# The last expert's down matrix in four loads, its token products moved, and four unread products ahead of the first wait

## What is computed

```python
def expert_choice_ffn(h, router_w, wg, wu, wd):
    ...
    a = jnp.einsum('becd,edf->becf', xs, wg)
    u = jnp.einsum('becd,edf->becf', xs, wu)
    o = jnp.einsum('becf,efd->becd', jax.nn.silu(a) * u, wd) * gate[..., None].astype(h.dtype)
    ...
for l in range(DEPTH):
    ...
    x = x + merged @ w_out[l]
    x = x + expert_choice_ffn(rms_norm(x, norm2_w[l]), router_w[l], ...)
```

## Time and profile before

| | |
|---|---|
| median of 3 runs | 2001.66 us (2000.48 to 2001.76) |
| profiled execution, its own time | 2003.29 us |
| its span, first to last instruction | 2001.5 us |
| mean granted TensorE clock | 0.891 of full |
| PE busy | 1563.8 us, 78% of the span |
| moved by DMA | 644.57 MB, 322 GB/s over the span |

### The profile page before, as it was taken

The page is one execution under the profiler, slowest core; times in us unless marked ns, Lnnn a source line. Parts: engine busy times, 40 slices in busy tenths (PEclk is TensorE's granted clock), DMA queues, the critical chain, the costliest instruction groups (busy, mean ns, idle before and its releaser), DMA issues.

```text
span 2001.5 us, 22268 instructions
## 1 busy us (share of the span) xinstructions
PE 1563.8 (78%) x9588; PEld 879.5 (44%) x9588; DVE 560.0 (28%) x1073; ACT 286.2 (14%) x600; POOL 45.7 (2%) x24
## 2 busy tenths in 40 slices
PE   8999999876576665676799999998765765666767
PEld 5687688432232232222256877884222221322322
DVE  3654771211111111111136547712111111111211
ACT  3233210110000000000132332101100100000010
POOL 0300000000000000000002000000000000000000
PEclk9999999898788887888899999998886878877888
DMA  7522055699999999999966221545999999999998
GB/s 294 227 89 84 1 230 206 250 393 425 432 428 433 435 427 434 434 430 411 423 218 231 85 84 40 237 181 244 437 431 426 432 436 428 430 434 430 431 419 341
DMA packets 26135, 644.57 MB, mean 322 GB/s; under 512 B 2864, under 2 KB 3888, under 8 KB 6320
## 3 DMA queue, kind: packets, MB, share of 16 engines
q1 hardware_dynamic: 24976, 638.47, 75.7%
q10 hardware_dynamic: 1056, 4.53, 0.8%
HBM read 641.94 MB, written 1.05 MB: 321 GB/s over the span
## 4 chain that ended last, share of the span: by engine, by line
PE 51%; DMA 45%; issue 1%; DVE 1%; ACT 1%; DVEq 0%; SPq 0%; ACTq 0%
DMA region<-w_down_dram 41%; PE ps L872 10%; PE ps L487 7%; PE ps L554 6%; PE ps L694 6%; DMA region<-w_down_last_dram 3%; PE ps L767 3%; PE ps L824 2%; PE ps L515 2%; PE ps L677 1%; PE ps L630 1%; PE ps L577 1%; PE ps L532 1%; PE ps L666 1%; PE ps L814 1%
## 5 line engine op out<-in xcount | busy, mean ns | idle before, releaser
L824 PE MATMUL ps<-ring,region 128*32 128x384 f32 (+1 forms) x2944 | 292.1, 531 | 184.9 <-DMA ring<-w_gbu_dram 184.9
L872 PE MATMUL ps<-region,late 128*32 128x512 f32 x1320 | 205.2, 742 | 124.1 <-DMA region<-w_down_dram 121.3
L824 PEld LDWEIGHTS ps<-ring,region 128*32 128x32 f32 x2944 | 120.1, 123 | 351.7 <-DMA ring<-w_gbu_dram 202.3
L487 PE MATMUL ps<-xnT,ring 128*128 128x256 f32 x768 | 178.3, 380 | 4.3 <-DVE region L1148 2.6
L1486 DVE TENSOR_TENSOR region<-region,ps 128x256 f32<-128x256 f32 x32 | 13.5, 421 | 549.7 <-PE ps L824 549.7
L872 PEld LDWEIGHTS ps<-region,late 128*32 128x32 f32 x1320 | 50.9, 133 | 257.5 <-issue 156.5
L487 PEld LDWEIGHTS ps<-xnT,ring 128*128 128x128 f32 x768 | 140.7, 190 | 23.8 <-DVE region L1148 4.4
L890 PE MATMUL ps<-region 128*128 128x512 f32 x256 | 124.3, 617 | 27.7 <-ACT region L1128 21.6
L554 PE MATMUL ps<-xnT,ring 128*128 128x256 f32 x512 | 115.8, 381 | 0.0
L1500 DVE TENSOR_TENSOR x<-x,ps 128x512 f32<-128x512 f32 x128 | 88.0, 688 | 83.0 <-PE ps L890 83.0
L1497 DVE COPY region<-ps 128x512 f32<-128x512 f32 x32 | 22.1, 692 | 314.8 <-PE ps L872 314.2
(11 more groups left out here) (204 smaller groups left out, 1482.1 us busy)
## 6 DMA issues: line engine op xcount, KB each, us to landing
region<-w_down_dram SPq DMA_DIRECT2D x28, 5632.0 KB, 32.9
ring<-w_gbu_dram SPq DMA_DIRECT2D x30, 4928.0 KB, 32.7
region<-w_ga_dram SPq DMA_DIRECT2D x14, 6336.0 KB, 36.8
ring<-w_ga_dram SPq DMA_DIRECT2D x12, 6336.0 KB, 34.8
ring<-units_dram SPq DMA_DIRECT2D x28, 2048.0 KB, 8.4
region<-units_dram SPq DMA_DIRECT2D x6, 2048.0 KB, 12.1
ring<-w_ga_dram SPq DMA_DIRECT2D x2, 4288.0 KB, 13.6
region<-w_down_dram SPq DMA_DIRECT2D x4, 2048.0 KB, 10.7
```

The costliest lines, as they stand in the source:

```text
L487: m = mm(bank(b % 2, S), unit8(n)[:, i, j * P:(j + 1) * P], xnT[:, i], start=i == 0, stop=i == DB - 1)
L824: m = mm(bank(b, QW[j], rows=CAP, row0=CAP * j), xs[:, i, q * CAP:(q + 1) * CAP], w[i][:, j * FT:j * FT + QW[j]], start=i == 0, stop=i == ...
L872: m = mm(bank(c, rows=CAP, row0=CAP * j), hT[:, b * P + CAP * j:b * P + CAP * (j + 1)], wd[:, CT * b + j, c * 512:(c + 1) * 512], start=b ...
```

## The change

The 11 tiles of half 0 arrive in two loads, of 6 and 5 tiles, and PE waits for the second one between its sixth and seventh tile. The 8 and 3 tiles of half 1 arrive as before, under other semaphores (`wd_in[2]`, `wd_end_in`). The token products of half 0 stand after tile 4 of half 1 and no longer after tile 7. Four products of a constant by the identity, 128x256 each, into a PSUM bank that nobody reads again for this expert, stand ahead of the waits for `hT_dve` and for the first load.

```diff
-                        for b, (c0, c1) in enumerate(((0, NF_TILES), (NF_TILES, 2 * NF_TILES - 3), (2 * NF_TILES - 3, 2 * NF_TILES))):
+                        for c0, c1, arrived in ((0, 6, wd_in[0]), (6, NF_TILES, wd_in[1]),
+                                                (NF_TILES, 2 * NF_TILES - 3, wd_in[2]),
+                                                (2 * NF_TILES - 3, 2 * NF_TILES, s["wd_end_in"])):
                             cols = slice(c0 * HW, c1 * HW)
-                            sp.dma_start(R[:, cols], w_down_last[L, :, cols]).then_inc(wd_in[b], 16)
+                            sp.dma_start(R[:, cols], w_down_last[L, :, cols]).then_inc(arrived, 16)
...
                         m.then_inc(s["hT_psum"], 1)
+                        if last and q == GROUP - 1:
+                            for _ in range(4):
+                                mm(bank(3, S), ident, cst[:, 0:S], start=True, stop=True)
 
                         pe.wait_ge(s["hT_dve"], n + 1)
...
-                    tiles(0, 0, NF_TILES).then_inc(s["o_half_psum"], 1)
+                    tiles(0, 0, 6)
                     pe.wait_ge(wd_in[1], 16 * (L + 1))
-                    tiles(1, 0, NF_TILES - 3)
+                    tiles(0, 6, NF_TILES).then_inc(s["o_half_psum"], 1)
+                    pe.wait_ge(wd_in[2], 16 * (L + 1))
+                    tiles(1, 0, 5)
                     pe.wait_ge(s["gselT_act"], n + 1)
                     pe.wait_ge(s["o_act"], n + 1 + FREE)
                     for t in range(SB):
                         to_tokens(n, t, t, 0)
-                    pe.wait_ge(wd_in[2], 16 * (L + 1))
+                    tiles(1, 5, NF_TILES - 3)
+                    pe.wait_ge(s["wd_end_in"], 16 * (L + 1))
                     tiles(1, NF_TILES - 3, NF_TILES).then_inc(s["o_psum"], 1)
```

More of the change, by code:

```diff
@@ L232, in build @@
         wd_last = R[:, 0:NF_TILES * D].rearrange("p (c r d) -> p c r d", c=2, r=NF_TILES)
-        names = """one_dve consts_in dft_in vec_in fvec_in qkw_in filt_in decay_in wqb_in wgbu_in wga_third_in wu_tail_in out_done
+        names = """one_dve consts_in dft_in vec_in fvec_in qkw_in filt_in decay_in wqb_in wgbu_in wga_third_in wu_tail_in wd_end_in out_done
         norm1_rms r_dve r2_dve xT_psum xw_dve xw_act r_psum xnT_dve lat_psum lat_rms lat_ready latT_psum latT_dve latT_act
```

## The result

The changed kernel took 2005.14 us (median of 20 runs, 2000.40 to 2010.47), the kernel before 2001.30 us (median of 20, 1996.29 to 2003.50): ratio 1.002, 95% interval 1.0013 to 1.0027. 3.84 us slower was measured, 3.35 forecast. The runs of the changed kernel spread over 10 us, those of before over 7.

A forecast was written before the change was run, and what follows sets the result against it. The experts are paced by the weights' DMA; each layer's end is set by half 1's arrival and PE's work behind it. 0.85 + 0.1 + 1.6 + 0.8 = 3.35 us on the median 2001.66 gave 2005.0 us, range 2001.6 to 2007.4.

The forecast's parts named there:

- The four loads cost nothing in the stream: Last expert's down loads: first six tiles land 3.1 us earlier, half 1 lands as before; cost 0.
- Rival 3: Load stream, last expert: the cut load brings half 1 1.4 us later per layer, 2007.8 us in all; chance 0.03.
- The unread products: Ahead of half 0: four products take 1.73 us at full clock, hold the tiles back 1.2 us, cost nothing at the end.
- The extra round: Behind half 1's arrival: four rounds of tiles for three, + 0.855 us, 5.70 in all; + 0.85 us in layer 0.
- Rival 4: Behind half 1's arrival: the two rounds of tiles 5 to 10 overlap, layer 1 gains 0.7 us, 2000.9; chance 0.03.
- Layer 1's + 0.1: Behind half 1's arrival in layer 1: 5.58 us before, 5.70 after at full clock, so + 0.1 us.
- Where the stall goes: PE's stall moves between half 0 and half 1, 2.7 to 3.1 us; lost clock then costs 1.6 (layer 1), 0.8 (layer 0).
- the clock is full throughout in both layers: Sign that the forecast is wrong; it expected half clock between half 1's arrival and DVE's copy in at least one layer.
- rival 1: The clock survives both stalls between the halves; only the round is left, 2001.66 + 0.95 = 2002.6 us; chance 0.22.
- 1.6 and 0.8: Us of clock loss behind half 1's arrival: 1.6 in layer 1, 0.8 in layer 0, where the stall is shorter.
- The sum: Both layers' ends: 0.85 + 0.1 + 1.6 + 0.8 = 3.35 us, added to the median 2001.66.

The follow-up runs named there:

- the second profile: Profile from an unedited repeat: of the kernel before (2001.09 us) under Layer 1's + 0.1, of the changed kernel (2005.01 us) under Where the stall goes.
- filler: Six more unread 128x256 products put into the changed kernel between half 0's last tile and the wait for half 1; 1998.65 us with them in both layers.

## Why the prediction was right, step by step

- **The four loads cost nothing in the stream.** Right. The gap from the first to the second landing in the profile after is 27.6 + 0.4 - 24.9 = 3.1 us for the 1280 KB, as worked out; half 1 lands 32.0 us after its issue, 32.4 before. Rival 3 is out. The 2.0 us that it names from the Trainium skill ("DMA: Bandwidth & Descriptors", section "Anatomy of one DMA") stand there for DMAs that GPSIMD issues; these are SP's, and no run shows such a part for one load more in a row.
- **The unread products.** Right: about 1.7 us (1978.75 to 1980.43 in the profile after), hidden. Leaving them out gained nothing, and the stall between the halves stayed as long.
- **The extra round.** The mechanism was right; 5.70 against 4.88 is 0.82 us a layer, 0.855 was forecast. Rival 4's overlap of rounds did not happen.
- **Layer 1's + 0.1.** This term was too small as a mean. It took from the first profile that before loses 0.74 us there; the second profile has none of it, and then the round costs 0.82 in layer 1 as well.
- **Where the stall goes.** Right as a mechanism, and the heart of it. The stall came out at 3.0 us in both layers (2.7 and 3.1 forecast). One loss was forecast at 1.6 us and measured 1.5 to 1.7. But the forecast also said that it would be wrong if the clock is full throughout in both layers, and the profile after shows just that, rival 1's case. Only the second profile has a loss, so of the changed kernel's own four ends one lost it. That losses are usual rests on the variants: in the profiles without a filler between the halves, and with half 0 done early, there are 14 such ends, the changed kernel's four among them; 10 lost 1.5 to 1.7 us, four lost nothing. Two of the 10 stand behind stalls of 2.0 us, the other 12 ends behind 3.0 to 3.3. With a filler there are six, and none lost any. Ten in fourteen makes 1.2 a layer, 2.4 in all; I had put 1.6 and 0.8, the same sum.
- **The sum.** 0.82 + 2.4, and between 0.1 and 0.8 for layer 1, is 3.3 to 4.0; measured were 3.84 and 3.1. That it meets the forecast this closely is partly luck: the share of 10 in 14 is that of other kernels too, the same losses left no mark on the median of the unread products alone, and two executions of one kernel differ upstream of both ends by up to 5 us, more than the whole sum.

What the forecast left out: that what PE does at layer 0's end can go along with a shorter time between the ends. It counted layer 1's stretch as passed through whole. For the change itself no profile shows a difference there: 954.4 and 955.3 us for the changed kernel, 953.9 and 956.2 before.

## What stays open

"Between" took 950.9 to 956.2 us in 14 profiles, two of them of before (953.9 and 956.2), for the same code. The three shortest (950.9, 951.1, 951.1) are the three that have six fillers in layer 0, the next (952.7) has fillers there too; the ten others are 953.9 to 956.2. So what PE does at the end of layer 0 goes along with a gain of some 3 us in layer 1's experts. That fits fillers bringing the time below before, which their own 1.6 us can't. I read it as when the clock's falls meet the products of the experts, but no run here moved that alone, and the rates above (432 and 430 GB/s) show only that the stream ran a little faster. Why it is the fillers' runs that have it was not settled, nor why the unread products alone came out level with before when both ends of their profile show the loss. Nor is it known how often the changed kernel itself loses the clock: two profiles show one loss in four ends. And what moves layer 0's half 1 from 993.1 to 998.3 us into the span, with identical code ahead of its last expert, was not looked into.

## What to carry to other kernels

Shortening work that lies hidden under a transfer gains nothing and moves the engine's stall to just ahead of the work that is not hidden; if the stall is long enough to cost the clock, the uncovered work pays. Look for what can be done in the stall, real work first (here the token products) and unread products where there is none, measured out so that they end before the data arrive (here they once ended 1.9 us after). And where products of 32 columns share the array in rounds of four, cut a sequence only between rounds: the cut cost 0.82 us here, and five tiles took as long as eight (1.90 and 1.92 us).

## What the hardware showed unexpectedly

One kernel's executions differ by over 11 us (1999.72 to 2011.11 for the changed kernel in 11 runs), and the one that a profile caught was the quickest of 20; two profiles of the same program differ in whether a stall of 3.0 us is followed by half clock (5.71 and 7.38 us for the same work). A stall of 2.0 us was followed by it twice in two. A single profile shows what can happen; how often takes several, and medians of ten runs or more.
